# Latent chunks 1 and 2 of a product-key expert layer: from gathered u rows and one-hot weight tables to two streamed tables and a scattered weight table

## What is computed

```python
def chunk(x):                                    # x: 128 tokens x 1024
    q = (x @ w_q).reshape(128, 8, 2, 128)        # 8 heads, 2 halves
    s = einsum('chpd,hpnd->chpn', q, sub_keys)   # 128 keys per half
    st, it = top_k(s, 16)
    cand = st[:, :, 0, :, None] + st[:, :, 1, None, :]
    best, pos = top_k(cand.reshape(128, 8, 256), 16)
    eidx = ...                                   # 16384 experts = 128 * key 0 + key 1
    g = softmax(best)
    act = gelu(einsum('chkd,cd->chk', u_tab[eidx], x))
    return einsum('chk,chkd->cd', g * act, v_tab[eidx])
```

## Time and the profile before

| | |
|---|---|
| runs | 2457.95, 2461.22 and 2464.52 us, median 2461.22 us |
| span of the profiled execution | 2458.3 us |
| median over span | 2.9 us |
| instructions | 20346 |
| busy | DVE 76%, PE 72%, PE weight loads 44%, POOL 42%, ACT 21% |
| DMA | 753.43 MB, 306 GB/s over the span |
| of it, gathered by POOL | 536.94 MB (1024 rows) |

### The profile page before, as it was taken

How to read it: one execution, slowest core, us unless ns; L and a number is a source line. 1 busy time by engine, 2 the same in 40 slices (tenths; PEclk the granted TensorE clock), 3 DMA queues, 4 the chain that set the end, 5 groups by cost and what they waited for, 6 DMA issues and landing times.

```text
span 2458.3 us, 20346 instructions
## 1 busy us (share of the span) xinstructions
PE 1778.0 (72%) x6013; PEld 1073.5 (44%) x6013; DVE 1873.6 (76%) x3933; ACT 514.3 (21%) x1283; POOL 1037.4 (42%) x1028
## 2 busy tenths in 40 slices
PE   7799889889887989891334666689999996000185
PEld 3578744444356438451012333556666664000032
DVE  2451588756789466889999999888687987999955
ACT  0563116440024000110004655710000000000111
POOL 0000000115534342443774776334344446777674
PEclk9899999899999999996566877899999998555599
DMA  9785772349955695866998999589999999999997
GB/s 279 250 274 193 233 231 87 113 135 319 353 182 180 215 330 177 288 250 211 384 410 285 390 411 404 200 300 411 414 411 414 411 411 411 410 408 406 364 404 304
DMA packets 296873, 753.43 MB, mean 306 GB/s; under 512 B 21502, under 2 KB 141102, under 8 KB 296244
## 3 DMA queue, kind: packets, MB, share of 16 engines
q0 software_dynamic: 147456, 536.94, 57.3%
q1 hardware_dynamic: 149308, 215.20, 25.0%
HBM read 740.72 MB, written 11.33 MB: 306 GB/s over the span
## 4 chain that ended last, share of the span: by engine, by line
DVE 37%; PE 29%; DMA 16%; POOL 8%; issue 6%; ACT 2%; DVEq 0%; SPq 0%; ACTq 0%; POOLq 0%
PE bank L788 12%; PE pair L788 6%; DVE big L1552 5%; DVE attn L1552 4%; DMA ring_more<-in_peer_u_dram,eidx 4%; DMA attn<-in_peer_u_dram,eidx 4%; DVE work L1552 3%; PE bank L971 3%; POOL work L2118 2%; DVE ring_more L1552 2%; POOL attn L2118 2%; PE bank L761 2%; POOL big L2118 2%; DMA attn<-in_peer_v_dram,eidx 2%; PE bank L1019 1%
## 5 line engine op out<-in xcount | busy, mean ns | idle before, releaser
L1019 PE MATMUL bank<-big,work 128*128 128x512 f32 x176 | 110.6, 767 | 369.4 <-ACT work L1091 266.3
L788 PE MATMUL pair<-big 128*128 128x128 f32 (+1 forms) x1280 | 361.8, 440 | 9.1 <-DVEq L1421 6.2
L2118 POOL DMA_INDIRECT h_all<-in_peer_u_dram,eidx x109 | 122.0, 1119 | 577.9 <-DVEq L1987 352.6
L788 PE MATMUL bank<-big 128*128 128x512 f32 (+1 forms) x1056 | 310.9, 453 | 34.4 <-DVEq L1421 22.7
L1064 PE MATMUL bank<-h_all,big 128*128 128x512 f32 x608 | 266.8, 595 | 4.6 <-DMA h_all<-in_peer_v_dram 4.6
L788 PEld LDWEIGHTS pair<-big 128*128 128x128 f32 x1280 | 197.3, 194 | 160.9 <-issue 158.6
L788 PEld LDWEIGHTS bank<-big 128*128 128x128 f32 x1056 | 169.2, 199 | 172.4 <-issue 165.0
L2118 POOL DMA_INDIRECT attn<-in_peer_u_dram,eidx x166 | 163.1, 983 | 165.5 <-DVE dots L1552 97.9
L1019 PEld LDWEIGHTS bank<-big,work 128*128 128x128 f32 x176 | 38.1, 235 | 427.0 <-issue 394.9
L1552 DVE CUSTOM_DVE_ANT_0 attn<-attn,pair 128x1024 f32<-128x1024 f32 x166 | 199.5, 1219 | 25.3 <-DMA attn<-in_peer_u_dram,eidx 23.0
L1064 PEld LDWEIGHTS bank<-h_all,big 128*128 128x128 f32 x608 | 180.5, 297 | 86.7 <-DMA h_all<-in_peer_v_dram 5.4
(11 more groups left out here) (311 smaller groups left out, 3172.7 us busy)
## 6 DMA issues: line engine op xcount, KB each, us to landing
big<-in_w_in_dram SPq DMA_DIRECT2D x44, 1024.0 KB, 6.5
h_all<-in_peer_v_dram SPq DMA_DIRECT2D x76, 512.0 KB, 6.8
big<-in_w_ada_dram SPq DMA_DIRECT2D x24, 1024.0 KB, 8.1
big<-in_peer_w_q_dram SPq DMA_DIRECT2D x16, 1024.0 KB, 5.6
gf_row<-in_peer_v_dram SPq DMA_DIRECT2D x26, 512.0 KB, 6.8
work<-in_peer_v_dram SPq DMA_DIRECT2D x26, 512.0 KB, 6.8
big<-in_w_rnn_o_dram SPq DMA_DIRECT2D x8, 1024.0 KB, 7.9
big<-in_w_attn_o_dram SPq DMA_DIRECT2D x8, 1024.0 KB, 6.4
```

Of the source, the lines that this page charges most:

```text
L788: last = nc.tensor.matmul(u[:, 0:n], w[:, k, col:col + P], src[:, k, 0:n], start=(k == 0), stop=(k == KD - 1))
L1019: last = nc.tensor.matmul(psum[i][:, :], diag[:, (n - 1) % DIAGS, :], ring[r][:, i * 512:(i + 1) * 512], start=(k == first_by_tensor[c]), ...
L2118: g.indirect_dma_start(dst, None, ins["peer_" + table][0], bass.IndirectOffsetOnAxis(ap=eidx[:, c, k:k + 1], axis=0)).then_inc(landed, 16)
```

## The change

Both tables are now streamed for chunks 1 and 2, and nothing is gathered for them.

- **Products.** SP loads u block n (128 experts x 1024) into one of two buffers. PE transposes it (8 transposes), ACT moves it from PSUM (2 x 128 x 512), PE multiplies it with the 256 tokens of both chunks (8 matmuls of 128 x 256), and ACT applies gelu and keeps the 128 x 256 result. There is room for 48 of them; 44 blocks are done ahead of the sums.
- **Weight table.** A DRAM table `w_flat` of 16384 experts x 256 tokens (16.8 MB) is zeroed by 32 DMAs that POOL issues early in phase 0. When two heads of a chunk are routed, POOL scatters their softmax weights into it, one indirect DMA with add for each slot: 128 single floats. Before the 16 scatters of the next head POOL waits until those of the head before have landed. It is 256 scatters in all.
- **Sums.** When all have landed, SP loads the 128 KB block n of the weight table, DVE multiplies it with the kept gelu block (`weigh`), and PE adds 4 matmuls of 128 x 512 with v block n.
- **Rows.** `turns` holds 592 rows: 80 v rows of chunk 0, all u and v rows of chunks 3 and 4. All of them go to DVE. The ring has 5, then 7, 9 and 10 buffers, where it had between 6 and 23.
- **Searches.** Chunk 2's top-k search is now inside phase 1's score loop too. `one_hots`, `weights`, `diags` and the trip through `w_later` are gone.

```diff
-    RING = 29
+    RING = 10
...
+    AHEAD_U, KEPT, U_BUFS, V_BUFS, W_BUFS, M_BUFS = 44, 48, 2, 4, 3, 2
+    EXPERTS = NKEY * NKEY
+    ZEROS = EXPERTS * TOKENS // (P * D)
...
+        return [0, 1, 2, 3, 4] + [5, 6] * (turn >= BESIDE) + [7, 8] * (turn >= C3_ROUTED) + [9] * (turn >= C4_ROUTED)
...  (SP)
+            for n in range(AHEAD_U + U_BUFS):
+                load_u(n)
+                if n == AHEAD_U // 2:
+                    sp_.wait_ge(pair_ready, PAIRS + 1)
+                    for i in range(V_BUFS):
+                        load_v(i)
+            for i in range(len(DENSE)):
+                sp_.wait_ge(scattered[i], 16 * SLOTS)
+            for n in range(W_BUFS):
+                load_w(n)
+            for n in range(NKEY):
+                if AHEAD_U + n + U_BUFS < NKEY:
+                    load_u(AHEAD_U + n + U_BUFS)
+                if n + W_BUFS < NKEY:
+                    load_w(n + W_BUFS)
+                if n + V_BUFS < NKEY:
+                    load_v(n + V_BUFS)
...  (PE)
+            def sums(n):
+
+                pe.wait_ge(m_ready, n + 1)
+                pe.wait_ge(v_in[n % V_BUFS], 16 * (n // V_BUFS + 1))
...
+            turn_u(0)
+            for n in range(AHEAD_U):
+                if n + 1 < AHEAD_U:
+                    turn_u(n + 1)
+                products(n)
+            for n in range(NKEY):
+                if AHEAD_U + n < NKEY:
+                    turn_u(AHEAD_U + n)
+                sums(n)
+                if AHEAD_U + n < NKEY:
+                    products(AHEAD_U + n)
...  (DVE)
+            def weigh(n):
+
+                if n >= M_BUFS:
+                    dve.wait_ge(v_used, n - M_BUFS + 1)
+                dve.wait_ge(g_ready, n + 1)
+                dve.wait_ge(w_in[n % W_BUFS], 16 * (n // W_BUFS + 1))
+                V.tensor_tensor(m_buf[n % M_BUFS], g_buf[n % KEPT], w_buf[n % W_BUFS], ALU.mult).then_inc(m_ready, 1)
+
+            def spent(us):
+
+                clock[0] += us
+                while made[0] < NKEY and clock[0] >= ALONE_US + (WORK - ALONE_US) * sums_at(made[0]) / sums_at(NKEY):
+                    weigh(made[0])
+                    made[0] += 1
...  (POOL)
+            g.memset(zero, 0.0).then_inc(zero_ready, 1)
+            pool.wait_ge(ada_ready, len(ada_first))
+            pool.wait_ge(zero_ready, 1)
+            for z in range(ZEROS):
+                g.dma_start(w_zero[z], zero).then_inc(zero_in, 16)
...
+            def scatter(i, h):
+
+                if h % 2 == 0:
+                    pool.wait_ge(pair_ready, PAIRS * i + h // 2 + 1)
+                if h:
+                    pool.wait_ge(scattered[i], 16 * TOPK * h)
+                for k in range(h * TOPK, (h + 1) * TOPK):
+                    g.indirect_dma_start(w_flat, bass.IndirectOffsetOnAxis(ap=widx[:, i, k:k + 1], axis=0),
+                                         gw[:, DENSE[i], k:k + 1], None, compute_op=ALU.add).then_inc(scattered[i], 16)
+
+            rows(0, BESIDE)
+            pool.wait_ge(zero_in, 16 * ZEROS)
+            for h in range(PH):
+                scatter(0, h)
+            for h in range(PH):
+                scatter(1, h)
+                rows(BESIDE + BESIDE_HEAD * h, BESIDE + BESIDE_HEAD * (h + 1))
+            rows(BESIDE + BESIDE_HEAD * PH, len(turns))
```

More of the change, by code:

```diff
@@ L300, in hybrid_step @@
[L300 to L306, removed]
-    def open_slots(turn):
[L310 to L324, removed]
+    U3, U4, V4 = step_start[1:]
@@ L333, in hybrid_step @@
         landings.append(16 * fills[r])
[L334 to L338, removed]
+    sum_rows = {c: [n for n, (table, c_, k) in enumerate(turns) if table == "v" and c_ == c] for c in (0, C3, C4)}
+    finals = [0, C3, C4, *DENSE]
+    gelus = [0, C3, C4]
+    softs = [0, *((c, p) for c in DENSE for p in range(PAIRS)), C3, C4]
     RING0 = 5
@@ L715, in _ @@
+            for i in range(1, NCH):
                 store(i)
@@ L1711, in topk, with settle @@
                 link(V.max_index(ti[:, 8:16], tv[:, 8:16], cut_))
[L1713 to L1718 removed]
+            def settle(c, pair, between):
                 h = 2 * pair
@@ L2086, in _, with sums_at @@
-            dve.wait_ge(final_in, 48)
-            final(0, wk(4, 2))
-            step_end(C3)
-            for pair in range(1, PAIRS):
-                n_rows = share(SLOTS // 2, pair - 1, PAIRS - 1)
-                route(C4, pair, lambda i: rows(share(n_rows, i, PARTS)))
-            rows(SLOTS // 2)
+            PART_US, ROW_US = (1.8, 1.8, 1.8, 1.8, 4.3, 5.3, 2.8), 1.3
+            BOTH_US, SUM_US = 8.2, 3.5
+            def sums_at(n):
+                both = NKEY - AHEAD_U
+                return BOTH_US * min(n, both) + SUM_US * max(n - both, 0)
@@ new lines, in rows_beside, with beside, between @@
+            def rows_beside(n):
+                for _ in range(n):
+                    rows(1)
+                    spent(ROW_US)
+            def beside(n_rows):
+                def between(i):
+                    spent(PART_US[i])
+                    rows_beside(share(n_rows, i, PARTS))
+                return between
+            pair_ids(C1, PAIRS - 1)
+            for pair in range(PAIRS):
+                best_of_64(C1 + 1, 2 * pair)
+                before[0] += 5.0
+                pair_diffs(C1 + 1, pair)
+                pair_ids(C1 + 1, pair)
+                before[0] += 7.0
+                pair_weights(*((C1 + 1, pair - 1) if pair else (C1, PAIRS - 1)))
```

1041 lines of the change are left out of this document (455 added, 586 removed).

## The result

| | |
|---|---|
| before | 2457.95 to 2464.52 us, median 2460.21 us (4 runs) |
| after | 2751.17 to 2760.87 us, median 2754.15 us (4 runs) |
| ratio | 1.119, 95% interval 1.1175 to 1.1212 |
| forecast | 2514 us, range 2430 to 2640 us |

The change makes the kernel slower by 12%, 294 us. Slower was forecast, with a chance of 0.72; the size was missed by 240 us, and the time lies outside the range.

The account below looks back on a forecast made before the run. POOL's scatters were to hold rows back to 1430 us, then mainly DMA bounds: first weigh at 1480 us, end at 2496, plus 15 for zeros and 2.9 around the span, 2514 us; range 2430 to 2640.

Parts of the forecast that it names:

- the price of a scatter: On POOL before the first weigh: each of 256 scatters starts 1.24 us after the last, as a 128-index fetch does.
- first scatter, without the zeros: End of the score loop: chunk 1's first pair has its softmax weights at 1067 us, so POOL can start.
- the zeros: From about 57 us: 16.8 MB of zero writes push back weight tiles, 15 us, bounds 0 and 41.
- first scatter to last landing: On POOL: 256 scatters 317 us, 24 rows between heads 30, waits 14; landed at 1430 us.
- last landing to first weigh: 24 more v rows 30 us, landing 7, add_sums 4, a search and five u rows 9; weigh at 1480 us.
- first weigh to the end of the span: Three stretches of 236, 578 and 189 us, 17 off, 8 more, then 22 at the end; ends at 2496 us.
- Rival 3: POOL's scatters dearer: 2581 us at 1.5 us each, 2831 at 2.48; DMA would need over 155 ns an element; chance 0.17.
- The signs of being wrong: Scatters nearer than 1.0 us, weigh 1 before 1420 us, or PE never pausing after 1480 us.
- PE ahead: Before the first weigh: 44 blocks of 4.33 us, 191 us, done at 1318 us in PE's idle time, at no cost.
- Rival 4: From weigh 28 to 84 PE bounds if its mean clock is below 0.75; 2806 us at 0.50; chance 0.08.
- The 8 us for the weight blocks' 1 KB pieces: After the first weigh: weight blocks move at 319 GB/s at full share, costing 8 us more.
- Rival 2: Between 1067 and 1430 us POOL's scatters are cheap: 2437 us at 0.94 us each, at most down to 2364; chance 0.20.

Follow-up runs that it names:

- experiment 1: The changed kernel with its 256 scatters writing their floats instead of adding them: 2606.25 us.
- experiment 7: The changed kernel with the 32 zero DMAs issued behind fetches of chunk 0's rows, from a 1 KB tile, instead of early: 2736.61 us.
- experiment 12: The changed kernel with scatters without add, zeros behind chunk 0's fetches and the first weigh behind 66 rows, on another chip: 2713.87 us.
- experiment 6: The changed kernel with 22 instead of 44 blocks of products ahead of the sums: 2796.87 us.
- experiment 5: The changed kernel with all 256 scatters left out and the wait for each pair of heads kept: 2424.23 us.
- experiments 1 to 5: Single edits to the changed kernel: no add, chunk 2's scatters out, more rows between heads, zeros paced, no scatters: 2606.25, 2533.35, 2752.89, 2754.93, 2424.23 us.
- experiment 3: The changed kernel with six rows instead of three behind each head of chunk 2's scatters: 2752.89 us.
- experiment 2: The changed kernel with chunk 2's 128 scatters left out and the rows behind each head kept: 2533.35 us.

## Why the prediction was wrong

The step that failed is the price of a scatter: "A scatter has 128 indices too, and I take the same 1.24 us." It was 1.85 us. That is 156 of the 240 us; the other 84 lie in the other terms, and all of these were too short as well. With the scatters at the price of the forecast (experiment 1) the kernel takes 2606 us, inside the range and 92 us over the sum. The terms, forecast and measured:

| term | forecast | measured | missed by |
|---|---|---|---|
| first scatter, without the zeros | 1067 us | 1080 us (experiment 7) | 13 |
| the zeros | 15 us | 22 us (experiment 7) | 7 |
| first scatter to last landing | 363 us | 1102 to 1633, 531 us | 168 |
| last landing to first weigh | 50 us | 1633 to 1702, 69 us | 19 |
| first weigh to the end of the span | 1016 us | 1049 us | 33 |

- **The scatters.** 256 x 0.61 = 156 of the 168 us are the spacing; the other 12 are mostly scatters that took up to 2.6 us (their mean is 1.58, not 1.54), and 16.2 us of waits for landings where 14 were forecast. Experiment 1 shows on the same chip that the add is the cause: without it they are 1.26 us apart and the kernel takes 148 us less. On another chip the same edit won 6 us (experiment 12), because there it slowed the other engines. Rival 3 held this outcome at 0.17, with 2581 us for 1.5 us a scatter and 2831 for 2.48; my range ended at 1.7. (By its sum 1.85 us give 2670 us; the other terms are the rest.) "Against: POOL's row does not depend on what DMA does" was no argument about another form of DMA: POOL's own instruction took 0.58 us more with add, and the trace doesn't show what it does in them. The signs of being wrong that the prediction names are all for the faster side; a scatter over 1.7 us should have been one.
- **What DMA does per element** is not what counted. The Trainium skill, "DMA: Bandwidth & Descriptors", section "Specifications", has transfers under 512 B done as read-modify-write. No run here shows whether they are. The traces show small packets at 46 ns with add and 12 ns without; with nine packets an engine that is 0.41 us in each 1.85, so POOL, not DMA, set the pace: 46 ns is well under the 155 ns that rival 3 needed.
- **The zeros** cost within the bounds of 0 to 41 us. The mechanism, bytes that push back weight tiles, held: pacing them in the same stretch won nothing, and moving them to a free one won 18.
- **PE ahead.** Forecast 191 us for 44 blocks and no cost; measured 194 us (1156 to 1351), hidden under the scatters. The rule that transposes do not engage the full clock ("TensorE: Matmul & The Clock Gate", "Part 4: PE-mode transpose", of the Trainium skill) would have made it an estimated 229 us. This trace does not agree: the granted clock was 1.00 over the stretch, and the 8 transposes between matmuls took 0.88 us, against 0.87 in the earlier trace rows. The score loop, freed of the zeros, ended at 1129 us (1127 forecast).
- **Rival 4, the clock**, did not come: 0.91 in 1922 to 2514 us, with PE pausing in each block.
- **Last landing to first weigh.** Three of the 24 rows that the prediction puts between the heads stand behind the last scatter, so 27 v rows of chunk 0 follow it and not 24. POOL needed 47 us for them (1632.7 to 1680.1 us), 10 of which it waited for buffers that DVE had not freed. DVE was the later one: but for 0.3 us it worked without a wait from 1644 us to the first weigh, on these rows and on two parts of the routing of chunk 3, which it had not reached before because it waited for chunk 0's rows (28.6 us before the row at 1637 us).
- **From the first weigh on** DMA bounds, as forecast: 220 + 592 + 213 us against 236 + 578 + 189, less 9. Experiment 6 shows it from the other side: 11.5 MB more cost 39 to 43 us, not the 95 of PE's blocks. The 33 us too little are mostly in the last part, where DMA had a share of 0.93 and I had taken 1.03. (The 8 us for the weight blocks' 1 KB pieces are 9 to 12 us by the prediction's own numbers, 13.1 to 16.8 MB at 319 instead of 410 GB/s.)
- **The faster side.** Rival 2 gave 2364 us at best. Experiment 5 shows 2424 with no scatters at all. That is this order's floor, 1.5% under the first chip's kernel before and 4.4% under that of its own chip, because the stretch behind the first weigh is 1049 us in the changed kernel and 1051 to 1056 in experiments 1 to 5.

## What to carry to other kernels

What a DMA costs POOL depended here on its form more than on its count of indices: a fetch of 128 rows of 4 KB holds POOL for 0.94 us, a write of 128 single floats for 0.96, the same with add for 1.54. When one queue feeds both the DMA engines and the step that all others wait for, putting its rows in another place in front of that step changed nothing (experiment 3); fewer (experiment 2) or cheaper instructions (experiment 1) did. And before the price of a new step is argued, leave the step out: here that bounds this arrangement at 1.5% or 4.4%, by the chip of the comparison. Last, an edit's effect belongs to the chip that it was measured on until a second one has shown it: leaving out the add was worth 148 us on one and 6 on another.

## What was not expected of the hardware

- An indirect write of 128 single floats is 32 packets, with add 144, and an adding packet takes 46 ns of a DMA engine against 12 ns. POOL is held for 1.54 us by the adding one and for 1.41 us by one of 64 floats, but for 0.94 us by a fetch that is 144 packets as well.
- While 16.8 MB of zeros that were issued at once were in the DMA engines, the small save of the adaLN rows held SP's next tile for 24 us; with the zeros paced it was 5.
- Plain scatters every 1.26 us left the other engines alone on one chip and slowed all of them on two others. One and the same kernel took 110 us longer on one of these.
